# Query products ahead of the latent and pool state turns in a two-layer pool/MLA decoder step

## The reference

```python
h = _rmsnorm(x, g_attn) * (1 + sc1) + sh1
proj = h @ w_in            # split: cq (768), ckv (256), kr (32), u (1024), gates (2048)
q = (_rmsnorm(cq, g_q) @ w_uq).reshape(B, S, 16, 64 + 32)
q_nope, q_rope = q[..., :64], _rope(q[..., 64:], pos)
latent = concat([_rmsnorm(ckv, g_kv), _rope(kr, pos)])     # output: new_latent
a_out, pool_new = _pool_mixer(u, pool_prev, ...)           # pool_new, output: last 15 rows of u
# attention with q and latents, then
x = x + g1 * ((sigmoid(gA) * a_out + sigmoid(gB) * b_out) @ w_out)
```

## Time and profile before

| | |
|---|---|
| median of 3 runs | 2315.89 us (2315.88 to 2316.04) |
| profiled execution, its own time | 2315.47 us |
| its span, first to last instruction | 2313.3 us |
| TensorE matmuls busy | 2232.8 us, 97% of the span |
| ACT / DVE / POOL busy | 38% / 50% / 29% |
| mean granted TensorE clock | 0.986 of 2.4 GHz |
| mean DMA traffic | 100 GB/s |

### The profile page before, as it was taken

The page is one execution under the profiler, slowest core; times in us unless marked ns, Lnnn a source line. Parts: engine busy times, 40 slices in busy tenths (PEclk is TensorE's granted clock), DMA queues, the critical chain, the costliest instruction groups (busy, mean ns, idle before and its releaser), DMA issues.

```text
span 2313.3 us, 42666 instructions
## 1 busy us (share of the span) xinstructions
PE 2232.8 (97%) x16207; PEld 1998.5 (86%) x16207; DVE 1158.3 (50%) x1827; ACT 876.3 (38%) x1874; POOL 664.5 (29%) x320
## 2 busy tenths in 40 slices
PE   6998999999999999999999899999999999999998
PEld 5898997557788999998988899965667989999998
DVE  4442653844345666651153608457444466666433
ACT  4222225832233555541132222267222345555311
POOL 0322443400022333333322244332000323333332
PEclk9999999999999999999999899999999999999999
DMA  8543332033332222236435243211332422222322
GB/s 294 169 144 78 87 82 68 19 104 109 87 130 81 82 82 82 82 100 186 157 118 170 76 90 82 82 44 53 93 107 56 156 63 82 82 82 82 92 84 74
DMA packets 338277, 230.67 MB, mean 100 GB/s; under 512 B 62732, under 2 KB 321605, under 8 KB 338140
## 3 DMA queue, kind: packets, MB, share of 16 engines
q1 hardware_dynamic: 335938, 224.01, 33.6%
q10 hardware_dynamic: 2202, 4.79, 0.6%
HBM read 223.15 MB, written 5.60 MB: 99 GB/s over the span
## 4 chain that ended last, share of the span: by engine, by line
PE 91%; ACT 3%; DVE 2%; SPq 2%; issue 1%; DMA 1%; DVEq 0%; ACTq 0%
PE PS L1510 60%; PE PS L1478 6%; PE PS L1895 5%; PE PS L1941 5%; PE PS L1527 3%; PE PS L1735 2%; PE PS L1838 2%; PE PS L1561 1%; ACT prob L749 1%; PE PS L1814 1%; PE PS L1791 1%; SPq L365 1%; PE PS L1889 1%; PE PS L1864 1%; DVE xn L1050 0%
## 5 line engine op out<-in xcount | busy, mean ns | idle before, releaser
L952 POOL TENSOR_TENSOR wlo<-raw,whi 128x1024 fp32r<-128x1024 f32 (+1 forms) x252 | 594.2, 2358 | 1537.8 <-ACT whi L540 1537.8
L540 ACT ACTIVATE whi<-raw 128x1024 fp32r<-128x1024 f32 (+1 forms) x252 | 258.7, 1026 | 939.7 <-PE PS L1510 815.4
L1510 PE MATMUL PS<-h_hi,whi 128*128 128x288 f32 x2496 | 538.0, 297 | 1.0 <-issue 1.0
L1510 PE MATMUL PS<-h_hi,wlo 128*128 128x288 f32 x2496 | 534.5, 295 | 0.0
L1510 PE MATMUL PS<-h_lo,whi 128*128 128x288 f32 x2496 | 534.4, 295 | 0.0
L1510 PEld LDWEIGHTS PS<-h_hi,whi 128*128 128x128 f32 x2496 | 402.5, 188 | 8.9 <-issue 8.5
L1510 PEld LDWEIGHTS PS<-h_hi,wlo 128*128 128x128 f32 x2496 | 402.8, 188 | 0.0
L1510 PEld LDWEIGHTS PS<-h_lo,whi 128*128 128x128 f32 x2496 | 402.7, 188 | 0.0
L1411 DVE TENSOR_SCALAR conv<-zext,convp 128x592 f32<-128x592 f32 x88 | 153.8, 1748 | 134.9 <-ACTq L866 134.5
L1510 PE MATMUL PS<-act_hi,whi 128*128 128x288 f32 x704 | 152.8, 298 | 0.0
L1510 PE MATMUL PS<-act_lo,whi 128*128 128x288 f32 x704 | 150.8, 295 | 0.0
(11 more groups left out here) (278 smaller groups left out, 3341.7 us busy)
## 6 DMA issues: line engine op xcount, KB each, us to landing
raw<-w_up SPq DMA_DIRECT2D x88, 512.0 KB, 3.8
pages<-cache_latent SPq DMA_DIRECT2D x256, 144.0 KB, 2.1
raw<-w_in SPq DMA_DIRECT2D x64, 512.0 KB, 4.0
ada_ring<-w_ada SPq DMA_DIRECT2D x41, 512.0 KB, 4.8
raw<-w_down SPq DMA_DIRECT2D x32, 512.0 KB, 3.7
ada_next<-w_ada SPq DMA_DIRECT2D x17, 512.0 KB, 4.2
ada_first<-w_ada SPq DMA_DIRECT2D x16, 512.0 KB, 10.0
raw<-w_out SPq DMA_DIRECT2D x16, 512.0 KB, 3.9
```

The costliest lines, as they stand in the source:

```text
L540: nc.scalar.activation(whi[:, slot, 0:width(u)], raw[:, slot, 0:width(u)], ACT.Copy).then_inc(hi_ready.sem, 1)
L952: nc.gpsimd.tensor_tensor(wlo[:, slot, 0:n], raw[:, slot, 0:n], whi[:, slot, 0:n].bitcast(F32), ALU.subtract).then_inc(lo_ready.sem, 1)
L1510: r = mm(PS[0:m, 2 * (j % 2) + half, 0:HT], w, o[:, k0 + k, half * HT:half * HT + HT], start=(first and k == 0 and part is whi and o is xh ...
```

## The change

TensorE starts the query products right behind u's last tile, with the four rope tiles. The units are renumbered (rope 16 to 19, plain 20 to 27), and SyncE loads them in that order. The first query tile is written to banks 6 and 7, so that it needs no free pair. The latent turns stand behind the second rope tile and use banks 4 to 7 (only the fifth group waits for a copy), the pool state turns behind the third. ACT does its copies and stores at the same places and waits for the stores after the fourth rope tile, ahead of the plain ones.

```diff
@@ units @@
-U_QN, U_QR, U_GATE, ... = 16, 24, 28, ...
+U_QR, U_QN, U_GATE, ... = 16, 20, 28, ...
@@ loads_before, width @@
-        return sum(2 if U_QN <= w < U_QR else 4 if U_QR <= w < U_GATE else 1 for w in range(u % 2, u, 2))
+        return sum(4 if U_QR <= w < U_QN else 2 if U_QN <= w < U_GATE else 1 for w in range(u % 2, u, 2))
...
-        if U_QN <= u < U_GATE:
+        if U_QR <= u < U_GATE:
@@ SyncE: the loop of the rope parts (4 loads a unit) now ahead of that of the plain parts (2 loads) @@
+                with sp.Fori(0, 2) as i:
...
                 with sp.Fori(0, 4) as i:
...
-                with sp.Fori(0, 2) as i:
...
@@ ACT @@
-                for n in range(5):
...
-                act.wait_ge(last_ev.sem, last_ev.at(l, 1))
...
+                def to_qr(f, s):
+                    banks = PS[:, 6:8, 0:HT] if f == 0 else bank_pair(s)
+                    nc.scalar.activation(tile_of(qr, f), banks, ACT.Copy).then_inc(free["uq"].sem, 1)
+
+                def latent_rows():
+                    for n in range(5):
+                        act.wait_ge(lat_T.sem, lat_T.at(l, n + 1))
+                        m = 128 if n < 4 else TS
+                        nc.scalar.activation(lat_rows[0:m, n, :], PS[0:m, 4 + n % 4, 0:LAT], ACT.Copy).then_inc(lat_ev.sem, 1)
+                    act.wait_ge(lat_ev.sem, lat_ev.at(l, 5))
...
+                def pool_state_rows():
+                    act.wait_ge(last_T.sem, last_T.at(l, 1))
+                    nc.scalar.activation(pool_rows[0:120, 0], PS[0:120, 4:6, :], ACT.Copy)
+                    nc.scalar.activation(pool_rows[0:CTX, 1], PS[0:CTX, 6:8, :], ACT.Copy).then_inc(last_ev.sem, 1)
+                    act.wait_ge(last_ev.sem, last_ev.at(l, 1))
...
+                for f in range(4):
+                    tile(U_QR + f, to_qr, f)
+                    if f == 1:
+                        latent_rows()
+                    if f == 2:
+                        pool_state_rows()
                 act.wait_ge(last_out.sem, last_out.at(l, 32))
                 act.wait_ge(lat_out.sem, lat_out.at(l, 32))
...
                 tiles(l, U_QN, 8, to_qn)
-                tiles(l, U_QR, 4, to_qr)
@@ TensorE @@
-            def products(slot, nk, xh, xl, k0, j, first=True, last=True, m=128):
+            def products(slot, nk, xh, xl, k0, j, first=True, last=True, m=128, pairs=2):
...
-                                r = mm(PS[0:m, 2 * (j % 2) + half, 0:HT], w, o[:, k0 + k, half * HT:half * HT + HT],
+                                r = mm(PS[0:m, 2 * (j % pairs) + half, 0:HT], w, o[:, k0 + k, half * HT:half * HT + HT],
...
-                pe.wait_ge(root.sem, root.at(l, 3))
-                pe.wait_ge(ckvn.sem, ckvn.at(l, 1))
+                def latent_turns():
+                    pe.wait_ge(ckvn.sem, ckvn.at(l, 1))
+                    pe.wait_ge(free["uq"].sem, free["uq"].at(l, 1))
+                    for n in range(5):
+                        m = 128 if n < 4 else TS
+                        if n == 4:
+                            pe.wait_ge(lat_ev.sem, lat_ev.at(l, 1))
+                            pe.sem_inc(passed[2], 1)
+                        for c in range(KC):
+                            turn(PS[0:m, 4 + n % 4, 128 * c:128 * c + 128], ckv[:, c, 128 * n:128 * n + m], 128)
+                        turn(PS[0:m, 4 + n % 4, KVL:LAT], krope[:, 128 * n:128 * n + m], DR).then_inc(lat_T.sem, 1)
+
+                def pool_state_turns():
+                    pe.wait_ge(lat_ev.sem, lat_ev.at(l, 5))
+                    pe.wait_ge(last_ready.sem, last_ready.at(l, 1))
...
+                pe.wait_ge(cqn.sem, cqn.at(l, 1))
                 pe.wait_ge(mod_ev.sem, mod_ev.at(l, 5))
-                for n in range(5):
...
-                pe.wait_ge(cqn.sem, cqn.at(l, 1))
-                banks_free_of(l, "u")
-                dense(l, "uq", U_QN, 8, KQ, cq_hi, cq_lo)
-                dense(l, "uq", U_QR, 4, KQ, cq_hi, cq_lo, 8)
+                for f in range(4):
+                    use(l, U_QR + f)
+                    if f > 0:
+                        banks_free_of(l, "u", but=int(f == 1))
+                        pe.wait_ge(free["uq"].sem, free["uq"].at(l, f - 1))
+                    products(f % 2, KQ, cq_hi, cq_lo, 0, 3 if f == 0 else f, pairs=4 if f == 0 else 2).then_inc(unit_used.sem, 1)
+                    if f == 1:
+                        latent_turns()
+                    if f == 2:
+                        pool_state_turns()
+                dense(l, "uq", U_QN, 8, KQ, cq_hi, cq_lo, 4)
```

More of the change, by code:

```diff
@@ L55 @@
 U_CQ, U_KV, U_U = 0, 6, 8
-U_QN, U_QR, U_GATE, U_UK, U_UV, U_OUT, U_UP, U_DOWN, UNITS = 16, 24, 28, 46, 48, 50, 58, 102, 126
+U_QR, U_QN, U_GATE, U_UK, U_UV, U_OUT, U_UP, U_DOWN, UNITS = 16, 20, 28, 46, 48, 50, 58, 102, 126
 GATE_UNITS = (("a", 0), ("a", 1), ("pool", 0), ("a", 2), ("a", 3), ("b", 0), ("b", 1), ("b", 2), ("b", 3), ("pool", 1),
@@ L432, in _ @@
                 w_uq = A["w_uq"].rearrange("a (k p) (h n) -> p a k h n", p=128, n=DN + DR)
+                with sp.Fori(0, 2) as i:
+                    for s in range(2):
+                        dst = raw[:, s, 0:768].rearrange("p (k h n) -> p k h n", k=KQ, h=4)
+                        sp.wait_ge(lo_ready.sem, lo_ready.at(l, U_QR + 2 * i + s - 1))
+                        for j in range(4):
+                            sp.dma_start(dst[:, :, j, :], w_uq[:, bass.ds(l, 1), :, bass.ds(8 * i + 4 * s + j, 1), DN:DN + DR]
+                                         .rearrange("p a k h n -> p (a k) (h n)")).then_inc(loaded[s].sem, 16)
                 with sp.Fori(0, 4) as i:
@@ L438, in _ @@
                             sp.dma_start(dst[:, :, j, :], w_uq[:, bass.ds(l, 1), :, bass.ds(4 * i + 2 * s + j, 1), 0:DN]
-                                         .rearrange("p a k h n -> p (a k) (h n)")).then_inc(loaded[s].sem, 16)
-                with sp.Fori(0, 2) as i:
[L441 to L445, removed]
                                          .rearrange("p a k h n -> p (a k) (h n)")).then_inc(loaded[s].sem, 16)
@@ L705, in to_qr @@
                 def to_qr(f, s):
-                    nc.scalar.activation(tile_of(qr, f), bank_pair(s), ACT.Copy).then_inc(free["uq"].sem, 1)
+                    banks = PS[:, 6:8, 0:HT] if f == 0 else bank_pair(s)
[6 more added lines that the diff above has]
+                    act.wait_ge(lat_ev.sem, lat_ev.at(l, 5))
+                    act.dma_start(O["lat_p"][bass.ds(l, 1)].rearrange("a b (n p) c -> p (a b n) c", p=128), lat_rows[:, 0:4, :]).then_inc(lat_out.sem, 16)
+                    act.dma_start(O["lat_s"][bass.ds(l, 1)].rearrange("a b s c -> (a b s) c"), lat_rows[0:TS, 4, :]).then_inc(lat_out.sem, 16)
+                def pool_state_rows():
[3 more added lines that the diff above has]
+                    act.wait_ge(last_ev.sem, last_ev.at(l, 1))
+                    act.dma_start(O["pool_s"][bass.ds(l, 1)].rearrange("a b r d -> (a b r) d"), pool_rows[0:120, 0].rearrange("p a b -> p (a b)")).then_inc(last_out.sem, 16)
+                    act.dma_start(O["pool_p"][bass.ds(l, 1)].rearrange("a b r d -> (a b r) d"), pool_rows[0:CTX, 1].rearrange("p a b -> p (a b)")).then_inc(last_out.sem, 16)
+                for f in range(4):
[4 more added lines that the diff above has]
+                        pool_state_rows()
+                act.wait_ge(last_out.sem, last_out.at(l, 32))
+                act.wait_ge(lat_out.sem, lat_out.at(l, 32))
                 tiles(l, U_QN, 8, to_qn)
-                tiles(l, U_QR, 4, to_qr)
                 def gate(kind, m, e):
@@ L1701, in _ @@
                         over_partitions(l, kv_sum[:, 0, :], 2)
-                pe.wait_ge(root.sem, root.at(l, 3))
-                pe.wait_ge(ckvn.sem, ckvn.at(l, 1))
-                pe.wait_ge(mod_ev.sem, mod_ev.at(l, 5))
-                for n in range(5):
[L1707 to L1721, removed]
-                pe.wait_ge(cqn.sem, cqn.at(l, 1))
-                banks_free_of(l, "u")
@@ new lines, in pool_state_turns @@
+                def pool_state_turns():
+                    pe.wait_ge(lat_ev.sem, lat_ev.at(l, 5))
+                    pe.wait_ge(last_ready.sem, last_ready.at(l, 1))
+                    for f in range(KD):
+                        o = 128 * (f % 4)
+                        turn(PS[0:NB * CTX, 4 + f // 4, o:o + 128], pool_last[:, f, CTX:], 128)
+                        r = turn(PS[0:CTX, 6 + f // 4, o:o + 128], pool_last[:, f, 0:CTX], 128)
+                    r.then_inc(last_T.sem, 1)
+                pe.wait_ge(cqn.sem, cqn.at(l, 1))
```

## The result

Four runs of the changed kernel gave a median of 2296.69 us (2295.41 to 2300.66), against 2315.89 before (2315.07 to 2316.04): ratio 0.9918, 95% interval 0.9905 to 0.9931, so 16 to 22 us faster. Forecast were 2294.4, range 2292 to 2301. The profiled execution took 2295.41 us with a span of 2293.3.

The account below looks back on a forecast made before the run. The prediction took TensorE as the bound, idle while waiting for DVE's normed latents. The two layers' stretches fall from 145.1 to 123.6 us, a gain of 21.5 us, giving 2294.4 us, range 2292 to 2301.

Parts of the forecast that it names:

- The bound and the wait: TensorE bounds the kernel; between u and the first latent turn it waits idle for DVE's normed latents, 6.22 us in layer one.
- The sum: From u's end to the first gate product, both layers: 145.1 us before, 123.6 after, a gain of 21.5 us.
- Products and seams: 432 query products take 57.1 us a layer; late starts of products after each block of turns add 0.2 us.
- Latent turns: Block after query tile two, its fifth group waiting for ACT's first evacuation: 2.45 us a layer.
- Pool turns: Sixteen pool state turns after query tile three, waiting for nothing: 2.05 us a layer.
- my own case: The change gains as summed, whole time 2292 to 2296 us, chance 81%.
- rivals 1 and 2: Turns pull the clock down, 6.6 us, about 2301 (10%); latents or evacuations late, 1 to 2 us, 2297 (5%).
- The stores' 3.2 us of cover: On ACT, first layer: last store lands at 198.6, ACT is next wanted at 201.8 when tile five ends.
- The DVE stretch I feared: A POOL subtraction slows DVE's last latent steps in layer two by 1.84 us, latents still ahead of the block.
- The rival's 1.25 us more for pool turns: Added time a layer for the pool state turns if turns pull the clock down; that rival had 10%.
- Rival 2: Latents late by a double DVE stretch, or ACT behind: 1 to 2 us in one or both layers, 2297 (5%).
- Rivals 3 and 4: First query tile doesn't start at u's end, 2315 (2%); clock stays down for tiles behind a block, 2371 (2%).

Follow-up runs that it names:

- e_fill: Kernel before the change, with 44 (second layer 50) useless matmuls filling TensorE's wait for the latents; ratio 0.997, stretches 6.9 us less than before.
- e_grouped: Changed kernel with the four krope turns behind the eight ckv turns instead of between them; ratio 0.9899, stretches 61.54 us in both layers.
- e_tile4: Changed kernel with both blocks of turns behind the fourth rope tile; ratio 0.9906, stretches 63.38 and 63.74 us.
- e_twice: Changed kernel with four latent groups and all sixteen pool turns each done twice; ratio 0.9935, stretches 65.49 us in both layers.
- e_tile1: Changed kernel with the latent turns one tile earlier, behind the first rope tile; ratio 0.9946, stretches 64.88 and 68.38 us.
- e_early: Kernel before, TensorE's order untouched, with DVE norming the latents behind the third of six cq tiles; ratio 0.9955, stretches 67.57 and 67.26 us.
- e_bank01: Changed kernel with its first rope tile in banks 0 and 1 instead of 6 and 7; ratio 0.9934, stretches 63.68 us in both layers.
- e_packed: Changed kernel with ten ckv turns in a row, then five krope turns, the fifth group in free columns; ratio 0.9899, stretches 60.54 and 60.55 us.

## Why the prediction was right

**The bound and the wait** stood as described: TensorE waited for DVE's latents, and e_fill names the releaser that the label "issue" hid. The first product follows u at once.

**The sum** was 21.5 us; the stretches show 22.0. Products and seams: 61.57 - 2.60 - 1.66 = 57.3, forecast 57.1 and 0.2. Latent turns 2.60 for 2.45: my working had the right floor for the wrong reason. I let the fifth group wait for ACT, with the four ahead of it at 1.5 us; they took 2.12 at 0.54 a group, since the change of shape costs time that rows of one shape don't show. ACT's copy would have come at the same moment, as e_grouped shows. Pool turns 1.66 for 2.05: 0.104 each, below both rates that I had taken (0.114 and 0.145). The two misses go opposite ways, 0.15 too little and 0.39 too much a layer, so the sum is nearer than its terms.

**Median.** The forecast 2294.4 was 2.3 below the first median, 2296.69. That median lies 0.7 above the 2292 to 2296 of my own case; only the part of the range that was meant for rivals 1 and 2 holds it, and neither of them came. The missing part is not in a term of the sum but in stages that vary from run to run; I had taken those as fixed. The later medians of the same kernel, 2295.02 and 2292.88, lie in 2292 to 2296. So that the first one fell inside the range stated is in part luck; the gain in the stretches is not.

**Covers.** SyncE's four small loads and POOL did not hold TensorE in the changed kernel. The stores' 3.2 us of cover held, and e_tile4 shows what is behind it. The DVE stretch I feared came in the second layer: the last latent step took 2.24 instead of 0.76 us beside POOL, and the latents were there at 1307.2, 0.9 before the block. It cost 1.48 us; I had costed 1.84, and my own two numbers (2.50 and 0.46) give 2.04. An earlier step, 1.83 us at 1300.39, was stretched too, but the kernel before had that as well (1.80 at 1309.62), so it was in the sum. Timelines of POOL and DVE:

```profile
1304.52 2.04 POOL L958 TENSOR_TENSOR wlo<-raw,whi 128x768 fp32r<-128x768 f32 x1 [2.91 <-ACT whi L540]
1304.93 2.24 DVE L1188 TENSOR_TENSOR ckv_lo<-ckv,ckv_hi 128x576 fp32r<-128x576 f32 x1
1307.28 0.22 DVE L1193 COPY pool_last<-uext 128x120 f32<-128x120 f32 x1
```

**Rivals.** The turns did not pull the clock down, and in e_twice twice as many didn't; but in e_tile1, in e_early and in one layer of e_tile4 the clock fell in the same turns with idle time ahead of or among them. Idle time does not always do it: with 0.36 and 0.49 us in e_fill and 0.72 in e_grouped the clock stayed at 1.00. The rival's 1.25 us more for pool turns at the lower clock was right (1.23 in e_tile4). The Trainium skill (TensorE: Matmul & The Clock Gate, Part 4: PE-mode transpose) says that a transpose doesn't count as busy the way a matmul does. What agrees with it here is that no stretch of turns brought the clock back (0.50 throughout in the kernel before); that turns without idle time would let it fall is not borne out, since in e_twice it stayed at 1.00. Rival 2 would have needed one more such stretch on DVE. Rivals 3 and 4 left no trace.

## What to carry to other kernels

Put independent dense work between a producer that is late and its small consumers on TensorE: it fills the wait, keeps the clock, and lets the engines that feed and empty those consumers catch up, which feeding the consumer earlier (e_early, with two banks) did not. Cost such a move by the stretch between two fixed points of TensorE's timeline; in the changed kernel it repeated to 0.01 us where the whole time varied by 9. And look at what a first tile's banks wait for: a pair of unused banks was a fifth of the gain.

## What the runs showed of the hardware

- Idle time and turns together could cost the clock where turns alone did not. Turns alone, 4.8 us: it stayed at 1.00 (e_twice). 1.88 us idle, then products: it stayed (e_bank01, both layers). 1.65 or 3.74 us idle, then turns: still 1.00 in the idle time, then it fell (e_tile1). 0.52 us idle between the two blocks of turns: it fell in one layer and not in the other (e_tile4). 0.36 and 0.49 us (e_fill) and 0.72 us (e_grouped) among turns: it stayed, in both layers. What decides between these cases no run shows. Idle time alone did it in the kernel before, with 6.2 and 7.0 us (0.87 and 0.73 over the stretch).
- A turn's time depends on its neighbour: 0.12 us in a row of ten of 128 rows, 0.08 in a row of five of 32 rows (e_packed); two and one of them by turns took 0.54, where these rates give 0.32. Not every change costs: the pool turns alternate between 120 and 15 columns and took 0.104 each.
- In this kernel 13.3 us of idle time cost 6.9 us more through the clock, at 1.2 GHz in the turns and the first products behind.
